# Weight chunks rounded, split and reloaded in two halves on Trainium2: a prediction and its test

## The reference

```
h = rmsnorm(x, gain)                  # 512 (or 256) rows of 1024
p = h @ w_in                          # and w_uq, w_ukv, w_o, ab_w_in, attn_w_qkv, ...
x = x + mixer(p) @ w_o
x = x + (silu(h @ w_gate) * (h @ w_up)) @ w_down      # D_FF = 2816
```

## Time and profile before

| | |
|---|---|
| median of three runs | 3534.76 us (3530.82 to 3542.27) |
| the profiled execution, its own time | 3537.52 us |
| its span, first to last instruction | 3535.7 us |
| mean granted TensorE clock | 0.93 |
| busy: PE, DVE, ACT, POOL | 3224.5, 1866.8, 1125.2, 1149.3 us |
| HBM read | 316.41 MB, 91 GB/s over the span |

### The profile page before, as it was taken

How to read it: one execution, slowest core, us unless ns; L and a number is a source line. 1 busy time by engine, 2 the same in 40 slices (tenths; PEclk the granted TensorE clock), 3 DMA queues, 4 the chain that set the end, 5 groups by cost and what they waited for, 6 DMA issues and landing times.

```text
span 3535.7 us, 41174 instructions
## 1 busy us (share of the span) xinstructions
PE 3224.5 (91%) x16508; PEld 2657.7 (75%) x16508; DVE 1866.8 (53%) x3026; ACT 1125.2 (32%) x1537; POOL 1149.3 (33%) x296
## 2 busy tenths in 40 slices
PE   5888999988888999997998989879999898979996
PEld 4645888866378788786888989768888776768885
DVE  3753778847645563764507754449665427341113
ACT  3342222123434432324326543232123324332221
POOL 2202334422036333323434443023434220124441
PEclk8898999988999999998999988679999789979998
DMA  6202445522034322223333332125553220113331
GB/s 112 66 13 65 127 144 180 171 68 66 13 93 142 96 81 87 72 72 107 107 90 108 108 96 72 60 72 166 168 172 114 69 70 1 29 53 98 96 95 48
DMA packets 481710, 324.36 MB, mean 92 GB/s; under 512 B 103616, under 2 KB 448832, under 8 KB 481008
## 3 DMA queue, kind: packets, MB, share of 16 engines
q1 hardware_dynamic: 477056, 310.37, 29.9%
q10 hardware_dynamic: 2656, 6.30, 0.5%
q0 software_dynamic: 1808, 5.05, 0.5%
HBM read 316.41 MB, written 5.24 MB: 91 GB/s over the span
## 4 chain that ended last, share of the span: by engine, by line
PE 77%; DVE 13%; ACT 4%; issue 2%; SPq 2%; POOL 1%; DMA 1%; DVEq 0%; ACTq 0%
PE G L2459 11%; PE G L2468 10%; PE G L2469 10%; PE G L2473 10%; PE G L2628 5%; PE G L2629 5%; PE G L2633 5%; PE G L2483 3%; PE M L2510 2%; PE M L2808 2%; DVE rstd L1389 1%; POOL WL L663 1%; ACT WH L714 1%; PE S L2459 1%; SPq L544 1%
## 5 line engine op out<-in xcount | busy, mean ns | idle before, releaser
L663 POOL TENSOR_TENSOR WL<-raw,WH 128x2048 fp32r<-128x2048 f32 (+1 forms) x260 | 1132.5, 4357 | 2200.3 <-ACT WH L714 2200.3
L714 ACT ACTIVATE WH<-raw 128x2048 fp32r<-128x2048 f32 (+1 forms) x260 | 468.1, 1801 | 685.3 <-PE G L2633 417.8
L2468 PE MATMUL G<-hH,WH 128*128 128x512 f32 x1520 | 595.6, 392 | 0.0
L2469 PE MATMUL G<-hL,WH 128*128 128x512 f32 x1520 | 592.8, 390 | 0.0
L2473 PE MATMUL G<-hH,WL 128*128 128x512 f32 x1520 | 360.1, 389 | 0.0
L2468 PEld LDWEIGHTS G<-hH,WH 128*128 128x128 f32 x1520 | 285.9, 188 | 60.1
L2469 PEld LDWEIGHTS G<-hL,WH 128*128 128x128 f32 x1520 | 286.0, 188 | 59.0
L2473 PEld LDWEIGHTS G<-hH,WL 128*128 128x128 f32 x1520 | 285.3, 188 | 59.2
L1452 DVE SCALAR_TENSOR_TENSOR acc<-adaw,cvec,acc 128x512 f32<-128x512 f32 x280 | 289.1, 1086 | 4.2
L2459 PE MATMUL G<-hH,WH 128*128 128x512 f32 (+1 forms) x448 | 172.8, 386 | 16.0 <-POOL WL L663 13.4
L2459 PE MATMUL G<-hL,WH 128*128 128x512 f32 (+1 forms) x448 | 171.3, 382 | 0.0
(11 more groups left out here) (657 smaller groups left out, 6413.3 us busy)
## 6 DMA issues: line engine op xcount, KB each, us to landing
raw<-ffn_w_in_in SPq DMA_DIRECT2D x264, 256.0 KB, 4.0
adaw<-ada_w_in SPq DMA_DIRECT2D x48, 1024.0 KB, 5.3
raw<-ab_w_in_in SPq DMA_DIRECT2D x128, 256.0 KB, 3.5
raw<-ffn_w_out_in SPq DMA_DIRECT2D x96, 256.0 KB, 3.5
raw<-w_gate_in SPq DMA_DIRECT2D x88, 256.0 KB, 3.4
raw<-w_up_in SPq DMA_DIRECT2D x88, 256.0 KB, 4.4
raw<-w_down_in SPq DMA_DIRECT2D x64, 256.0 KB, 3.4
raw<-w_in_in SPq DMA_DIRECT2D x40, 256.0 KB, 3.8
```

The lines of the kernel that those rows point to most:

```text
L663: nc.gpsimd.tensor_tensor(WL[c % 2][:, 0:size_of[c]], raw[c % 2][:, 0:size_of[c]], WH[c % 2][:, 0:size_of[c]].bitcast(F32), ALU.subtract)\
L714: nc.scalar.activation(WH[c % 2][:, 0:cols], raw[c % 2][:, 0:cols], ACT.Copy).then_inc(weights_hi, 1)
L2468: mm(dst, view(WH[c % 2], k), high, start=(k == 0 and not (joint and i)), stop=False)
L2469: mm(dst, view(WH[c % 2], k), low, start=False, stop=False)
```

## The change

Each chunk is handled as two parts. Part 0 holds the columns that the first DMAs bring, part 1 the rest: half and half with two DMAs each, but 512 and 1024 columns (three and six DMAs) for the `uq` chunks. Each `raw` buffer gets two landing semaphores. ACT issues two ACTIVATEs and POOL two TENSOR_TENSORs per chunk, each waiting for its own part alone. SP reloads part 0 as soon as POOL has read part 0 of chunk c - 2 (or both, where the cut lies further right than before), and then part 1. PE's waits name the second part of the same chunk, so they mean what they meant. No DMA, matmul or engine order is changed otherwise.

```diff
-        raw_loaded = [sem("raw_loaded0"), sem("raw_loaded1")]
+        raw_loaded = [[sem(f"raw_loaded{b}_{part}") for part in range(2)] for b in range(2)]
...
-        pieces_of = [PIECES] * (CHUNKS + 2)
+        pieces_of = [(PIECES // 2, PIECES // 2)] * (CHUNKS + 2)
+        cut_of = [cols // 2 for cols in size_of]
         for l in range(DEPTH):
             for n in range(2):
-                pieces_of[first[f"b{l}.uq"] + n] = 3 * QL // P
+                pieces_of[first[f"b{l}.uq"] + n] = (3, 6)
+                cut_of[first[f"b{l}.uq"] + n] = 1536 // 3
+            pieces_of[first[f"b{l}.in"] + 2] = (1, 3)
...
+                n = pieces_of[c][0]
+                for part, some in enumerate((pieces[:n], pieces[n:])):
+                    if c >= 2:
+                        sp.wait_ge(weights_lo, 2 * (c - 2) + (1 if part == 0 and cut_of[c] <= cut_of[c - 2] else 2))
+                    for dst, src in some:
+                        sp.dma_start(dst, src).then_inc(raw_loaded[c % 2][part], 16)
...
-                    pool.wait_ge(weights_hi, c + 1)
-                    nc.gpsimd.tensor_tensor(WL[c % 2][:, 0:size_of[c]], raw[c % 2][:, 0:size_of[c]], WH[c % 2][:, 0:size_of[c]].bitcast(F32), ALU.subtract)\
-                        .then_inc(weights_lo, 1)
+                    for part, cut in enumerate(parts(c)):
+                        pool.wait_ge(weights_hi, 2 * c + part + 1)
+                        nc.gpsimd.tensor_tensor(WL[c % 2][:, cut], raw[c % 2][:, cut], WH[c % 2][:, cut].bitcast(F32), ALU.subtract)\
+                            .then_inc(weights_lo, 1)
...
-                act.wait_ge(raw_loaded[c % 2], come(c))
                 if c >= 2:
                     act.wait_ge(pe_done, at("pe", f"used.{c - 2}"))
-                cols = size_of[c]
-                nc.scalar.activation(WH[c % 2][:, 0:cols], raw[c % 2][:, 0:cols], ACT.Copy).then_inc(weights_hi, 1)
+                for part, cut in enumerate(parts(c)):
+                    act.wait_ge(raw_loaded[c % 2][part], come(c, part))
+                    nc.scalar.activation(WH[c % 2][:, cut], raw[c % 2][:, cut], ACT.Copy).then_inc(weights_hi, 1)
...
-                pe.wait_ge(weights_hi, c + 1)
+                pe.wait_ge(weights_hi, 2 * c + 2)
...
-                pe.wait_ge(weights_lo, c + 1)
+                pe.wait_ge(weights_lo, 2 * c + 2)
```

More of the change, by code:

```diff
@@ L417, in build, with come, parts @@
         CHUNKS = len(size_of)
-        pieces_of = [PIECES] * (CHUNKS + 2)
+        pieces_of = [(PIECES // 2, PIECES // 2)] * (CHUNKS + 2)
+        cut_of = [cols // 2 for cols in size_of]
         for l in range(DEPTH):
             for n in range(2):
-                pieces_of[first[f"b{l}.uq"] + n] = 3 * QL // P
-        def come(c):
-            return 16 * sum(pieces_of[c % 2:c + 1:2])
+                pieces_of[first[f"b{l}.uq"] + n] = (3, 6)
+                cut_of[first[f"b{l}.uq"] + n] = 1536 // 3
+            pieces_of[first[f"b{l}.in"] + 2] = (1, 3)
+        def come(c, part):
+            return 16 * sum(n[part] for n in pieces_of[c % 2:c + 1:2])
+        def parts(c):
+            return (slice(0, cut_of[c]), slice(cut_of[c], size_of[c]))
         first_tile = [sum(QUARTERS[:q]) for q in range(len(QUARTERS) + 1)]
@@ L474, in load @@
             def load(c, pieces):
[L476 to L480, removed]
+                assert len(pieces) == sum(pieces_of[c])
+                n = pieces_of[c][0]
[4 more added lines that the diff above has]
+                        sp.dma_start(dst, src).then_inc(raw_loaded[c % 2][part], 16)
             def columns(c, w, c0, cols=2 * P):
```

## The result

The changed kernel takes **3518.1 us** (median of 6 runs, 3515.6 to 3522.7) where the kernel before took 3537.0 in the same session (6 runs): a ratio of 0.9944 with the interval [0.9933, 0.9956], 0.56% faster. I had forecast 3497, 1.07%. The wide range (3468 to 3526) held the result, but half of the gain did not come.

A forecast was written before the change was run, and what follows sets the result against it. PE, busy 91% of the span, bounds the kernel, so only its idle or low-clock time can pay; 19 + 8.7 + 8.3 + 4.2 + 1.9 - 4 = 38 us gives 3497 us against the median of 3534.8, range 3468 to 3526.

The forecast's parts named there:

- Column pass: Context's column pass, where PE waits for weights: 19 us gained, bounds 9 and 22.
- reload: Loading a chunk's buffer again: a half lands in about 4 us, a whole chunk in 6; PE is the limit next.
- earlier chain: From ACT's start through POOL: WL is whole 0.65 us sooner where only ACT's start counts.
- The rival in which ACT's order holds the pass: Column pass: rounding stays behind ACT's activation work, 9 us gained there, new catches eat DVE's gains; 3526 us, chance 0.07.
- Against it: POOL starts sooner and once more per chunk, catching free DVE instructions: 3 us lost, plus 1 for ACT's second fixed cost.
- kind 2: DVE instructions stalled in POOL's first 1.5 us, followed by more of their sort (rstd, pooling steps, modulation sums): 8.3 us gained.
- three kinds of DVE stalls: Stalled DVE instructions on the chain outside the column pass, 26 of 30, shortened by POOL's halves: 8.7, 8.3 and 4.2 us.
- kind 1: Five DVE instructions stalled in POOL's first 1.5 us, result wanted by another engine, end at 2.1 instead of 5.1: 8.7 us.
- Kind 3: Seven DVE instructions stalled in the later part of POOL's work end 0.6 us sooner each: 4.2 us gained.
- WL waits elsewhere: PE's waits for WL outside the column pass, three of them 0.65 us shorter each: 1.9 us gained.
- first rival: Only the weights come sooner, DVE's stalls stay as long: gain 19 us, 3516 us, chance 0.17.
- slower rival: POOL's 260 further starts catch 34 DVE instructions on the chain, costing 41 us against 21 gained: 3555 us, chance 0.06.

The follow-up runs named there:

- three versions with edits in the pass alone: Kernel before, with only the column pass and two chunks behind it by halves: everything, all but ACT's rounding, or all but loads; ratios 0.9931, 0.9968, 0.9981.
- pass-only version: Kernel before with loads, ACT and POOL by halves only in the column pass and the two chunks behind it: 3512.5 us, ratio 0.9931.
- second stretch: Kernel before with halves in the column pass and also from the context's output weights to its first gate/up chunks (1565 to 1900 us): 3512.6 us, 0.9930.

## Why half of the forecast gain did not come

**Column pass, 19 us forecast: right,** and by its own steps. 17.6 us came between 1045 and 1162 us: 2.9 up to the matmul at 1053.23 of before (2 forecast), 12.5 from there to the matmul at 1157.12 of before (15.4), 2.2 behind it (2). What I had split as reload (landing in 4 instead of 6) and earlier chain (0.65) are 10.0 and 7.8 us alone. That PE becomes the limit holds: POOL works 71 of the pass's 91.4 us. The rival in which ACT's order holds the pass is refuted, its wait fell from 3.21 to 1.03 us.

**The step that failed is "Against it": 3 us for all new catches,** and 1 for ACT. I had found eight DVE instructions on the chain that were free and began in the 0.85 us before a POOL start. A count over the whole chain of before gives 29, among them four FL, which began 0.68 us before POOL's start (one of them 0.18), and two c_FL, 0.63 before it. So the term was too small already in its count. Outside the pass 33 instructions are newly caught, with 59.9 us of surplus. A part of that, where the second half catches the next of a chain, stood inside the term for kind 2; the rest stood nowhere. Five times FL is on the changed kernel's chain and stopped (2.03, 1.81, 2.03, 2.03, 2.00 us), c_FL four times (1.69, 1.67, 1.67, 1.70); three of these nine were off the chain before, where I had not looked. The nine have 16.6 us. Not all of it is time lost: FL and c_lf, shown above, have 4.2 us together where c_m alone had 4.29. But the FL at 3457 us, where before had no stall, held PE for 1.36 us.

**The three kinds of DVE stalls, 8.7 + 8.3 + 4.2:** kind 1 was priced as if only the one stalled instruction mattered. Surplus before and after, at places of each kind:
- Kind 1 (another engine wants the result): qT had 3.94; now qT and the next instruction, vg, have 0.92 and 2.09: 0.9 gained where I had 2. hL at 1607 had 4.10, now two have 1.02 and 1.64: 1.4 instead of 2.7. The two in the recurrence (4.33 and 4.22) became five with 10.6, a loss of 2.0 where I had a gain of 2. The second half catches what follows, on kind 1 as well.
- Kind 2 (more of the same follow): rstd had 3.38, now 0.28 and 1.97: 1.1 where I had 0.8. The pooling steps had 3.20, now 1.14 and 2.10: nothing.
- Kind 3 (stopped late): pm had 2.05 and has 1.25: 0.8 where I had 0.6.

So kinds 2 and 3 were about of the right size where a place can be compared, kind 1 was far too high, and catches at new places ate most of the rest: outside the pass the surplus went from 92.3 to 85.0 us, and PE drew 1.5 us ahead, where I had 19 in sum. The last term, 1.9 for WL waits elsewhere, did not come either: they were 9.65, 3.76 and 0.63 and are 11.33, 3.72 and 0.21. The first of them varies between 7.05 and 11.76 over the kernels here, so its loss says little.

**The signs named ahead.** POOL has its 520 instructions, at 2.50 and 1.99 us with the DVE's turns in them (2.39 and 1.84 forecast). The longest surplus is 2.76 us where it was 4.33: "stalls of over 4 us remain" did not come, so the first rival's mechanism is wrong, though its 3516 us is the closest of my figures: that is luck. The median stalled instruction lasts 2.40 us (under 3 forecast). rstd waits 70.5 us (69 forecast). Of the feed-forwards, PE's stretches from 370 to 690 and from 2400 to 2700 us of before last as long as then, but that from 3160 to 3490 takes 331.6 us instead of 330.0, behind the caught FL: I had forecast 0.1% at most. Waits in the pass were to be under 5 us; its first, 4.95 before, is still 4.18, and with 1.03 and 1.99 the three sum to 7.2. Of its three stretches at the lower clock, which begin at 1049, 1097 and 1155 us in before, the first is still there and the other two are gone. The count of stalled instructions on the chain passed the 50 that I had set as the mark of the slower rival (57), yet nothing was lost: each was half as long. That rival had priced 34 new ones at 1.2 us, 41 in all; there are 33 with 59.9. It left out that the old ones shrink in exchange (92.3 to 29.8, and only 20 of the 29 are still on the chain, with 25.2). It was the right mechanism beside the forecast's, and I had treated the two as alternatives. They happen together, and nearly cancel.

## What to carry to other kernels

Where two engines exclude each other for whole instructions, cutting one's work in two halves each stall and doubles their number: price both, and look at the instructions that are free by a hair, off the chain too, above all when the cut also moves the start. Cut finer (four, eight) where the cutting engine has idle time. Where it nearly sets the pace, as in the pass, the limit comes sooner: there four parts were still 2.8 us ahead of before with nothing else changed, eight 0.5 behind. Here the places were apart, and treating them apart brought 1.2% instead of 0.6%. Splitting load, rounding and subtraction paid in the stage that waits for weights; elsewhere it brought 0.1% at most.

## What the runs showed of the hardware

**Strict turns.** After the change POOL's two halves run without a gap and one DVE instruction slips in between: FL above ends 0.55 us after POOL's first half (1404.73 against 1404.18), and c_lf, which starts at 1404.65, ends at 1407.25, 0.27 after the second (1406.98). Scans and the smallest instructions are stopped alike (before, the scan c_m at 1423.70 took 4.97 us instead of 0.68, and t_mids of 128x8 at 1873.66 took 4.33 instead of 0.17). That each of the two goes on after one instruction of the other, and so what cutting is worth, is shown by the rstd chain with eight parts: 0.98 and 1.04 us for each addition, 0.70 for a free one. The Trainium skill (SBUF — State Buffer, SBUF: two separate sides) states an exclusive lock, held for the whole instruction, which the trace bears out with 2.03 us lost by an instruction of 0.69. The page of the Trainium skill that I had weighed ahead of the runs (GPSIMD Engine Reference, Key points) says only that there is contention.

**The clock makes some microseconds without an edit.** The same 1212 matmuls of the latent recurrence in before, in the pass-only version (where nothing was changed there), and in the changed kernel:

```profile
2064.00:2285.00 221.00, 208.01 (x1212) 189.33 (x1213) 92.64 (x271) 64.87 (x82) 59.71 (x14) 0.76 0.23 74
```

```profile
2045.50:2259.60 214.10, 201.06 (x1212) 182.88 (x1213) 93.32 (x271) 64.96 (x82) 59.80 (x14) 0.79 0.24 76
```

```profile
2040.60:2265.80 225.20, 211.56 (x1212) 192.43 (x1213) 95.38 (x271) 66.24 (x96) 62.50 (x28) 0.74 0.22 73
```

DVE, ACT and POOL do the same work in the first two, and the stretch differs by 6.9 us with the granted clock, 0.76 and 0.79 on average between its two levels. From 1162 us on, where none of the three versions with edits in the pass alone has one, they drew 7.6, 3.7 and 5.8 us ahead. A difference of a few us between two single profiles of this kernel says nothing by itself; that is why the 5 us that I expected from the second stretch stay open, and why the verdicts above rest on the timed rounds. Whether these microseconds are chance or go with a kernel is not shown: all three drew ahead, and the timed gain of the pass-only version, 24 us, holds some 6 more than its pass.
